# A chunked RWKV-7 recurrence: half of the head pairs change array halves with each product

## What is computed

```python
def _rwkv7_scan(r, w, k, v, kh, a):
    z, t, h, n = r.shape
    ...
    def step(state, inp):
        r_t, w_t, k_t, v_t, kh_t, a_t = inp
        removed = jnp.einsum('zhvk,zhk->zhv', state, kh_t)
        state = (state * w_t[:, :, None, :] - removed[..., None] * (kh_t * a_t)[:, :, None, :]
                 + v_t[..., None] * k_t[:, :, None, :])
        return state, jnp.einsum('zhvk,zhk->zhv', state, r_t)
    _, y = lax.scan(step, jnp.zeros((z, h, n, n), jnp.float32), seq)
```

## Time and profile before

| | us |
|---|---|
| median of 3 runs (lowest, highest) | 2473.24 (2471.79, 2482.2) |
| the profiled execution, its time | 2481.17 |
| its span, first to last instruction | 2479.4 |
| the recurrence in it, first to last matmul | 232.9 (at 1630.9 to 1863.8) |
| mean granted TensorE clock of the span | 0.939 |

### The profile page before, as it was taken

How to read it: one execution, slowest core, us unless ns; L and a number is a source line. 1 busy time by engine, 2 the same in 40 slices (tenths; PEclk the granted TensorE clock), 3 DMA queues, 4 the chain that set the end, 5 groups by cost and what they waited for, 6 DMA issues and landing times.

```text
span 2479.4 us, 36641 instructions
## 1 busy us (share of the span) xinstructions
PE 2190.2 (88%) x15081; PEld 1454.2 (59%) x15081; DVE 842.2 (34%) x1598; ACT 499.8 (20%) x840; POOL 244.1 (10%) x223
## 2 busy tenths in 40 slices
PE   4988989998998898999689887569998689999995
PEld 3766757873776675884134455369993434444442
DVE  0256231001246522000307855644435412222224
ACT  1243300000234310000023112134330111111111
POOL 2256200000046500000000000100000000000000
PEclk9998898999999899999899987789999799999998
DMA  5421343444322153543652201000005299999993
GB/s 168 142 100 53 136 156 115 137 169 148 129 102 102 54 201 102 166 140 119 209 183 68 102 0 68 0 3 4 4 4 189 99 402 405 401 402 403 402 403 146
DMA packets 139367, 392.92 MB, mean 158 GB/s; under 512 B 16951, under 2 KB 64415, under 8 KB 127713
## 3 DMA queue, kind: packets, MB, share of 16 engines
q1 hardware_dynamic: 139233, 390.95, 42.3%
HBM read 389.88 MB, written 1.05 MB: 158 GB/s over the span
## 4 chain that ended last, share of the span: by engine, by line
PE 41%; DVE 6%; ACT 2%; DMA 1%; issue 1%; SPq 0%; POOL 0%; DVEq 0%; ACTq 0%; POOLq 0%
PE psum L2480 8%; PE psum L1163 8%; PE psum L1827 5%; PE psum L2504 4%; PE psum L1876 3%; PE psum L1187 2%; PE psum L2461 2%; PE psum L2531 2%; PE psum L1336 1%; PE psum L1855 1%; PE psum L2173 1%; DMA arena<-in_ex_up_dram 1%; DVE arena L1718 1%; PE psum L2492 1%; PE psum L2159 1%
## 5 line engine op out<-in xcount | busy, mean ns | idle before, releaser
L354 PE MATMUL psum<-arena,ring 128*128 128x256 f32 x1728 | 390.6, 387 | 8.2 <-ACT arena L647 4.8
L354 PEld LDWEIGHTS psum<-arena,ring 128*128 128x128 f32 x1728 | 335.9, 195 | 61.7 <-issue 6.8
L552 PE MATMUL psum<-arena,ring 128*128 128x256 f32 x1408 | 307.8, 380 | 2.0 <-ACT arena L580 2.0
L552 PEld LDWEIGHTS psum<-arena,ring 128*128 128x128 f32 x1408 | 267.8, 190 | 42.1 <-issue 2.7
L580 ACT ACTIVATE arena<-psum 128x512 f32<-128x512 f32 (+2 forms) x116 | 65.6, 566 | 593.6 <-PE psum L552 280.4
L1827 PE MATMUL psum<-arena 64*64 64x64 f32 (+1 forms) x3808 | 148.0, 228 | 20.6 <-DVE arena L2004 18.6
L1827 PEld LDWEIGHTS psum<-arena 64*64 64x64 f32 x3808 | 138.1, 136 | 23.1 <-DVE arena L2004 19.0
L566 PE MATMUL psum<-ring,arena 128*128 128x512 f32 x352 | 151.4, 592 | 0.0
L1163 PE MATMUL psum<-arena,ring 128*128 128x512 f32 (+2 forms) x432 | 144.1, 494 | 0.0
L1163 PEld LDWEIGHTS psum<-arena,ring 128*128 128x128 f32 (+1 forms) x432 | 82.1, 190 | 62.5 <-issue 56.3
L956 DVE TENSOR_TENSOR arena<-arena,psum 128x512 f32<-128x512 f32 x22 | 15.2, 690 | 303.3 <-PE psum L552 303.3
(11 more groups left out here) (381 smaller groups left out, 2749.1 us busy)
## 6 DMA issues: line engine op xcount, KB each, us to landing
ring<-in_w_in_dram SPq DMA_DIRECT2D x31, 2048.0 KB, 8.1
ring<-in_ffn_w_dram SPq DMA_DIRECT2D x46, 1024.0 KB, 6.1
ring<-in_ex_gate_dram SPq DMA_DIRECT2D x15, 2048.0 KB, 10.5
ring<-in_ex_up_dram SPq DMA_DIRECT2D x15, 2048.0 KB, 15.0
ring<-in_ex_down_dram SPq DMA_DIRECT2D x15, 2048.0 KB, 7.4
arena<-in_ex_gate_dram SPq DMA_DIRECT2D x15, 2048.0 KB, 11.0
arena<-in_ex_up_dram SPq DMA_DIRECT2D x15, 2048.0 KB, 15.5
arena<-in_ex_down_dram SPq DMA_DIRECT2D x15, 2048.0 KB, 17.3
```

The source lines that it names most:

```text
L354: ins = pe.matmul(bank[:, j, :], w[:, kc, c * P:(c + 1) * P], moving[:, kc, :], start=kc == 0, stop=kc == k - 1)
L552: ins = pe.matmul(bank[:, j, :], both[:, i * DC + kc, j * P:(j + 1) * P], K.xT[:, kc, :], start=kc == 0, stop=kc == DC - 1)
```

## The change

Of the four pairs the first two (`CROSSED`) now turn halves with each product: the head in the upper partitions has its result written to the lower ones and the other way round, which uses the upper right and lower left quadrants. The other two pairs stay straight. `quadrants` gives the order: for one crossed and one straight pair the two crossed matmuls and then the two straight ones, each of another quadrant. Since a crossed and a straight matmul would write the same partitions of one bank, a key now has two banks side by side (crossed pairs in the even one, straight ones in the odd one), and `wkv_groups` puts `None` after each key: 4 places instead of 8.

A head must lie in the same half as what it is multiplied with, so some things change with it:

- `iv` has a second term, the unit matrix times the inverse so far: VectorE could not add an inverse that lies in the other half. So each `iv` has 16 matmuls instead of 8, and `grow` is a copy. That is all of the 640 matmuls more: 4,208 instead of 3,568.
- `pw` of level 1, the second half of `t2` and the state's term of `y` and `st` stay straight for all pairs (`halves`).
- For `y` and `st` the crossed pairs' parts come out in two places (`side`, in both banks). VectorE adds them: three operations of half size instead of one for `y`, four for `st`, with waits between them. ScalarE drains `t2` by two operations instead of one.
- VectorE's `pairs` moves up, behind each direction's `inner`.

```diff
-    return keys
+    return [key for key in keys for key in (key, None)]
...
+def by_head(banks, n=CH):
+    return banks.rearrange("p b (u n) -> p (b u) n", u=2)[:, :, 0:n]
...
+def apart(banks):
+
+    return banks.rearrange("p b (u n) -> p b u n", u=2)[:, :, :, 2 * CH:3 * CH]
...
+CROSSED = HP // 2
+
+
+def quadrants(us=range(CROSSED)):
+
+    for u in us:
+        for h in range(2):
+            yield u, HEAD_ROWS[h], HEAD_ROWS[1 - h]
+        for h in range(2):
+            yield u + CROSSED, HEAD_ROWS[h], HEAD_ROWS[h]
+
+
+def halves(us=range(HP)):
+    return [(u, r, r) for u in us for r in HEAD_ROWS]
...
         pe.wait_ge(K.empty(key), K.empty_count(key))
-        bank = by_pair(K.bank(key), n * CH)
-        for u in range(HP):
+        bank = by_head(K.two_banks(key), n * CH)
+        for two in range(CROSSED):
             for i, (a, b) in enumerate(terms):
-                for r in HEAD_ROWS:
-                    ins = pe.matmul(bank[r, u, :], a[r, u], b[r, u], start=i == 0, stop=i == len(terms) - 1)
+                for u, r, out in quadrants([two]):
+                    ins = pe.matmul(bank[out, u, :], a[r, u], b[r, u], start=i == 0, stop=i == len(terms) - 1)
+        ins.then_inc(K.full(key), 1)
+
+    def with_state(key, terms, a, b):
...
+            for i, (x, y) in enumerate(terms):
+                for u, r, out in quadrants([two]):
+                    place = side[out, 0, u, :] if u < CROSSED else bank[out, u, :]
+                    pe.matmul(place, x[r, u], y[r, u], start=i == 0, stop=u < CROSSED and i == len(terms) - 1)
+            for u, r, out in halves([two + CROSSED, two]):
+                place = side[out, 1, u, :] if u < CROSSED else bank[out, u, :]
+                ins = pe.matmul(place, a[r, u], b[r, u], start=u < CROSSED, stop=True)
...
-                for u in range(HP):
-                    for r in HEAD_ROWS:
-                        ins = pe.matmul(bank[r, u, i, :], a[r, u], b[r, u], start=True, stop=True)
+                for u, r, out in quadrants() if n > 1 else halves():
+                    ins = pe.matmul(bank[out, u, i, :], a[r, u], b[r, u], start=True, stop=True)
...
-            each(("iv", n, c, z), 1, (zt_now, t.inv))
+            each(("iv", n, c, z), 1, (zt_now, t.inv), (ones, t.inv))
...
-            tt_op(t.s, by_pair(K.bank(key), CH), last.broadcast_to([P, HP, CH]), ALU.mult).then_inc(K.empty(key), 1)
...
+            dve.tensor_copy(s, moved_part).then_inc(link.sem, 1)
+            tt_op(t.s[:, CROSSED:], straight[:, CROSSED:], last[:, CROSSED:], ALU.mult)
+            dve.wait_ge(link.sem, link.count())
+            tt_op(s, s, kept_part, ALU.add).then_inc(link.sem, 1)
+            dve.wait_ge(link.sem, link.count())
+            tt_op(s, s, last[:, 0:CROSSED], ALU.mult).then_inc(K.empty(key), 1)
...
-        tt_op(t.inv, t.inv, by_pair(K.bank(key), CH), ALU.add).then_inc(K.empty(key), 1)
+        dve.tensor_copy(t.inv, by_head(K.two_banks(key), CH)).then_inc(K.empty(key), 1)
...
             if c < CHUNKS:
                 inner(c, z)
+                pairs(c, z)
...
-        if c < CHUNKS:
-            for z in range(ZS):
-                pairs(c, z)
```

More of the change, by code:

```diff
@@ new lines, in each @@
+        ins.then_inc(K.full(key), 1)
+    def with_state(key, terms, a, b):
+        pe.wait_ge(K.empty(key), K.empty_count(key))
+        banks = K.two_banks(key)
+        bank, side = by_head(banks, CH), apart(banks)
+        for two in range(CROSSED):
+            for i, (x, y) in enumerate(terms):
[5 more added lines that the diff above has]
+                ins = pe.matmul(place, a[r, u], b[r, u], start=u < CROSSED, stop=True)
@@ L1847, in turned @@
         v, kr = K.rv[:, :, at:at + CH], t.decayed(c, False)[:, :, 0, :]
[L1848 to L1852, removed]
-                for u in range(HP):
-                    for r in HEAD_ROWS:
-                        ins = pe.matmul(bank[r, u, i, :], src[r, u, :], one[r, :], start=True, stop=True)
-            ins.then_inc(K.full(key), 1)
+        key = ("t1", c, z)
+        pe.wait_ge(K.empty(key), K.empty_count(key))
+        bank = by_two(K.two_banks(key))
+        for i, src in enumerate((t.b, t.k)):
+            for u, r, out in quadrants():
+                ins = pe.matmul(bank[out, u, i, :], src[r, u, :], one[r, :], start=True, stop=True)
+        ins.then_inc(K.full(key), 1)
+        key = ("t2", c, z)
+        pe.wait_ge(K.empty(key), K.empty_count(key))
+        banks = K.two_banks(key)
+        bank, side = by_two(banks), apart(banks)
+        for u, r, out in quadrants():
+            pe.matmul(side[out, 0, u, :] if u < CROSSED else bank[out, u, 0, :], v[r, u, :], one[r, :], start=True, stop=True)
+        for u, r, out in halves():
+            ins = pe.matmul(side[out, 1, u, :] if u < CROSSED else bank[out, u, 1, :], kr[r, u, :], one[r, :], start=True, stop=True)
+        ins.then_inc(K.full(key), 1)
     def level(n, c, z):
@@ L1919, in outputs @@
             if c > 0:
-                terms += [(t.gr[:, :, 1, :], t.s)]
-            each(("st", c, z), 1, *terms)
+                with_state(("st", c, z), terms, t.gr[:, :, 1, :], t.s)
+            else:
+                each(("st", c, z), 1, *terms)
     for c in range(CHUNKS + 1):
@@ L2043, in outputs @@
             dve.wait_ge(K.full(key), K.full_count(key))
-            y = K.y_sum[:, :, at:at + CH]
+            straight, (moved_part, kept_part) = by_head(K.two_banks(key), CH), (apart(K.two_banks(key))[:, n] for n in range(2))
+            y, x = K.y_sum[:, CROSSED:, at:at + CH], K.y_sum[:, 0:CROSSED, at:at + CH]
             if c < LAT + LAT // 2:
-                dve.tensor_copy(y, by_pair(K.bank(key), CH)).then_inc(K.empty(key), 1)
+                dve.tensor_copy(x, moved_part).then_inc(link.sem, 1)
+                dve.tensor_copy(y, straight[:, CROSSED:])
             else:
```

51 lines of the change are left out of this document (35 added, 16 removed).

## The result

| | before | changed |
|---|---|---|
| median, us | 2477.58 (4 runs, 2471.79 to 2482.2) | 2502.84 (4 runs, 2501.26 to 2507.23) |
| profiled execution: its span, us | 2479.4 | 2500.0 |
| ahead of the recurrence, us | 1630.9 | 1627.7 |
| the recurrence, us | 232.9 | 254.9 |
| behind it, us | 615.6 | 617.4 |

The changed kernel is slower, at 1.0104 times the time of the kernel before (95% interval 1.0081 to 1.0128). The profiled executions differ by 20.6 us, and the recurrence alone takes 22.0 us more.

A forecast was written before the change was run, and what follows sets the result against it. Instruction supply was taken to bound the recurrence: 66.3 blocks x 3.85 us = 255.3, plus 1 us of waits, 256.3 against 232.9; 2473.24 + 23 = 2496 us (+0.9%), range 2465 to 2520.

The forecast's parts named there:

- The bound: Recurrence: TensorE's instruction supply decides, 66.3 blocks of 256 giving 255.3 us; chance 0.66.
- The price of a block: Recurrence: 3.85 us per 256 instructions, between 3.78 and 3.925 read from the earlier trace; own range 3.6 to 4.05.
- The page's rule: Skill page: blocks of 256 instructions are fetched ahead, the crossing "mostly hidden"; by that word the sum would be 2407 us.
- rival B: Recurrence: supply is not the bound; 147 us of work + 20 of VectorE waits, -66, 2407 us; chance 0.15.
- Four quadrants: Recurrence: all four quadrants work side by side, 14.6 ns a record; array work 147 us against 225.
- C: Recurrence: a floor for each record between 14.6 and 29.2 ns, whatever the quadrant; -34, 2440 us; chance 0.05.
- D: Recurrence: crossed and straight matmuls don't overlap, 262.4 us of work; +30, 2503 us; chance 0.08.
- rival E: Recurrence: with stalls filling 40%, its clock may fall from 0.99 to 0.5; +46, 2519 us; chance 0.06.
- the waits: TensorE in the recurrence: 133 waiting instructions, 105 fewer than before, counted as 0.4 block less.
- A term that was mis-sized: VectorE: Recurrence: five more operations per direction and chunk, some 20 to 30 us on VectorE; TensorE waits 1 us in all.
- The signs to look for: Recurrence: 65 to 67 packets, bursts of 2.3 us or less, "issue" stalls of 1.2 to 1.7 us, busy share toward 60%.
- The doubt that was left: Recurrence: 3.85 us was read where TensorE's work was about as long; wrong if packets come faster than every 3.5 us.

The follow-up runs named there:

- e1: The changed kernel without the unit-matrix term of `iv`; ratio 0.9932 to the kernel before, recurrence 218.5 us.
- e2: The changed kernel with all four pairs straight: same instructions on two quadrants instead of four; ratio 1.0109 to the kernel before, recurrence 264.76 us.
- e10: The changed kernel with both `pw` products of levels 1 to 4 as one matmul of 128 columns, 512 matmuls fewer; ratio 0.9953 to the kernel before.
- e7: The changed kernel without `iv`'s unit-matrix term, plus two waiting instructions at every fourth recurrence matmul; ratio 1.0221 to the kernel before, recurrence 291.5 us.
- run 12: Not a follow-up run: the words say that VectorE's four operations for `st` are executed 12 times inside the recurrence.
- e3: The kernel before with every recurrence matmul cut to 16 columns of 64 (32 of 128), ScalarE's copies at scale 0; 2667.53 us, recurrence 380.8 us.

## Why the prediction was right, point by point

- **The bound.** That blocks of 256 instructions come in 3.85 us, and that this and not the array would set the end, is what the changed kernel shows: 66 packets, 254.9 us against 256.3. e1, e2 and e10 each moved one side: ten blocks less gave 36.5 us, twice the array's time gave 9.8, eight blocks less at the same columns gave 36.3. What is shown is that the time goes with the number of instructions in blocks of 256, that TensorE's stalls over 0.8 us stand at the block's edge alone, and that these stalls end 1.20 to 1.57 us after an instruction packet has landed, so that what TensorE waits for there is its instructions. Why a packet starts when it does was not found. The time came out at 2502.84 us against 2496; 4.3 of the 6.8 us are the median of the kernel before, which stood at 2473.24 in the prediction and at 2477.58 with its fourth run.
- **The price of a block, right with some luck.** "0.25 us of each 3.925 is lost, which is the size of the stalls" misreads the eight blocks of the earlier trace rows. Only two of them end in a stall over 0.2 us, the first and the last; the others last 3.62 to 3.98 us, and one 4.76, as long as their matmuls take, of which 32 records are wide ones. So 3.85 rests on few starved blocks, in a kernel where supply and work were nearly level; single starved blocks of the changed kernel last 3.3 to 4.6 us, and it is their mean that is 3.83. The prediction's idea of a constant supply holds for this instruction stream; e7's blocks took 4.6 us.
- **The page's rule.** The Trainium skill's page "Runtime: NRT & Kernel Launch", section "Instruction fetch mechanics", calls the crossing "mostly hidden". The trace disagrees for matmuls as small as these: 73.9 us of "issue" in 255. e1 and e10, which got shorter with their blocks, speak against rival B too.
- **Four quadrants.** The prediction inferred them from the earlier trace rows; the bursts show them, with 14.6 ns a record. Rivals C and D are out: C by the bursts, D because a record in e2 takes 29 ns (0.93/32 us), twice as long.
- **The clock (rival E).** It moved, but not as a whole: granted 0.97 over the recurrence instead of 0.99. Where it was down, the stalls covered most of it. One such stretch of the changed kernel:

```profile
1637.50:1645.20 7.70, 5.58 (x252) 5.25 (x252) 2.63 (x6) 3.52 (x8) 0.00 (x0) 0.79 0.02 4
```

Two blocks in 7.70 us, which is again 3.85 each.
- **A step that was wrong, and small: the waits.** "133 waits" and "105 fewer, already in the count (0.4 block)". Both this and the description of the change are wrong. The changed kernel has 238 waiting instructions in the recurrence, as before: the order's listing names a semaphore once where two of its values are waited for. With 238 the count is 17,070, 66.7 blocks, and the sum 256.7 + 1.
- **A term that was mis-sized: VectorE.** Forecast 20 to 30 us more; its busy time rose by 6.3, from 93.27 to 99.52. Operations of half size took 277 to 293 ns, as estimated (rows below: busy us, mean ns, idle before). But the sum gave each of 8 chunks and 2 directions five more operations, 80 in all, while the four for `st` run 12 times and the three for `y` 7 times inside the recurrence (an eighth lies behind its last matmul): 50 were added (267 against 217 in the rows of the recurrence). The 0.1 us for each wait in the chain was too much: ahead of the 12 operations of L2128 VectorE stood idle 0.4 us in all. What TensorE waited for VectorE, 2.0 us, was near the 1 that was taken.

```profile
L2128 DVE TENSOR_TENSOR arena<-arena 128x128 f32<-128x128 f32 x12 | 3.5, 293 | 0.4
L2123 DVE COPY arena<-psum 128x128 f32<-128x128 f32 x12 | 3.5, 291 | 21.0 <-PE psum L1871 21.0
L2124 DVE TENSOR_TENSOR arena<-psum,arena 128x128 f32<-128x128 f32 x12 | 3.4, 280 | 0.0
L2126 DVE TENSOR_TENSOR arena<-arena,psum 128x128 f32<-128x128 f32 x12 | 3.3, 277 | 0.0
```

- **The signs to look for.** Bursts of 2.3 us or less: 2.2. Stalls of 1.2 to 1.7: up to 2.0. Busy share "toward 60": 70, as the records cover 178.5 us where the work was put at 147. Some 20 of these 31 us are the ends of the bursts: 126 records are 1.84 us by the price, and their records cover 2.21, since each lasts over 0.2 us by itself. The rest was not taken apart.
- **The doubt that was left.** A supply that is asked for more "might give more". It gave 3.85 us on average under full demand; e10 shows a lower mean, 3.73, and e7, with waiting instructions in every block, a higher one, 4.58.

## What to carry to other kernels

Count instructions as well as array time: where every float32 matmul is four instructions and lasts tens of ns, the supply of instructions (here 256 in 3.85 us, 15 ns each) can be the bound. Its signs are an "issue" stall in the middle of a group, at the same place of each 256 instructions, and an instruction packet that lands some 1.4 us before the stall ends. A change that halves the array's time by way of more, smaller instructions then loses; what pays is fewer instructions: wider matmuls, fewer weight loads, an addition moved to an engine with room. And a waiting instruction on a queue of small matmuls is not free, even when the semaphore has long had its value: it takes a place in a block, and in e7 the next block came later with such instructions in it.

## What the runs showed of the hardware that was not expected

- A stall at the edge of a block of 256 instructions ends 1.20 to 1.57 us after the end of a packet of 16,384 bytes (59 stalls of the changed kernel; 1.24 to 1.58 in 58 of e7). The packet takes 1.1 us and starts 1.34 us after the block's first instruction, or 2.11 in e7, where 28 waiting instructions lie in each block.
- A float32 matmul of 64x64 weights takes as long with 16 moving columns as with 64 at 1.2 GHz: 74 MATMUL records in 3.90 us in both, 53.4 ns a record over the whole of e3.
- With these short matmuls the granted clock stayed at 0.50 for 380 us, with TensorE's records back to back. Busy time of records doesn't tell which clock will be granted.
- Waiting instructions with nothing to wait for follow each other at 0.106 us in TensorE's queue, and begin only some 0.5 us before the last matmul ahead of them starts: 28 keep the weight loads waiting for 2.4 to 2.7 us.
